# mLSTM output gates projected channel-major in four HGRN heads and applied by VectorE after the result transposes

## What is computed

```python
z = rmsnorm(x, norm_mix_g)
proj = z @ w_in
(ml_qk, ml_v, ml_o, ml_g, hg_q, hg_ff, hg_fb, hg_i, hg_g, gate_m, gate_h) = split_cols(proj, IN_SPLITS)
...
y_m = (head_rmsnorm(h_fwd + h_bwd, ml_norm_g) * jax.nn.sigmoid(ml_o)).astype(dt)
...
merged = sigmoid(gate_m) * (y_m @ w_branch_m) + sigmoid(gate_h) * (y_h @ w_branch_h)
x = x + merged @ w_out
```

## Time and profile before

| what | value |
|---|---|
| median of 3 runs | 2597.02 us (2594.98 to 2597.72) |
| span of the profiled execution | 2591.9 us |
| median less span | 5.1 us |
| PE busy | 2549.5 us (98%), 13936 matmuls |
| DVE, ACT, POOL busy | 1608.1, 913.1, 708.4 us |
| granted TensorE clock, mean | 0.996 |

### The profile page before, as it was taken

How to read it: one execution, slowest core, us unless ns; L and a number is a source line. 1 busy time by engine, 2 the same in 40 slices (tenths; PEclk the granted TensorE clock), 3 DMA queues, 4 the chain that set the end, 5 groups by cost and what they waited for, 6 DMA issues and landing times. The chain is left out here.

```text
span 2591.9 us, 34942 instructions
## 1 busy us (share of the span) xinstructions
PE 2549.5 (98%) x13936; PEld 2210.0 (85%) x13936; DVE 1608.1 (62%) x1811; ACT 913.1 (35%) x1109; POOL 708.4 (27%) x689
## 2 busy tenths in 40 slices
PE   7999999999999999999999999999999999999998
PEld 7888888899999999888888889977798888888887
DVE  5675552577888778553544524333437998987557
ACT  6342222233333333332223533243323433433433
POOL 2033220022221111422331001167412565563001
PEclk9999999999999999999999999999999999999999
DMA  8323334333222323434343546145514132334755
GB/s 282 116 78 130 98 114 138 122 114 100 85 91 101 106 98 98 163 121 147 130 154 122 212 130 219 34 165 194 202 34 146 66 130 98 114 114 171 284 194 180
DMA packets 185008, 349.62 MB, mean 135 GB/s; under 512 B 10283, under 2 KB 114039, under 8 KB 184848
## 3 DMA queue, kind: packets, MB, share of 16 engines
q1 hardware_dynamic: 123104, 154.44, 18.1%
q0 software_dynamic: 32896, 118.44, 13.2%
q10 hardware_dynamic: 28848, 74.52, 7.7%
HBM read 241.10 MB, written 106.27 MB: 134 GB/s over the span
## 5 line engine op out<-in xcount | busy, mean ns | idle before, releaser
L2225 PE MATMUL ps<-whi,a_hi 128*128 128x256 f32 x1024 | 295.6, 289 | 0.0
L2225 PE MATMUL ps<-whi,a_lo 128*128 128x256 f32 x1024 | 290.1, 283 | 0.0
L2225 PE MATMUL ps<-wlo,a_hi 128*128 128x256 f32 x1024 | 290.1, 283 | 0.0
L2194 PE MATMUL ps<-a_hi,whi 128*128 128x512 f32 x608 | 248.8, 409 | 0.2 <-DVE a_lo L1550 0.2
L1531 DVE TENSOR_TENSOR wlo<-raw,whi 128x2048 fp32r<-128x2048 f32 x65 | 150.1, 2309 | 142.6 <-ACT whi L943 142.4
L2194 PE MATMUL ps<-a_hi,wlo 128*128 128x512 f32 x608 | 237.8, 391 | 0.0
L2194 PE MATMUL ps<-a_lo,whi 128*128 128x512 f32 x608 | 237.4, 390 | 0.0
L2225 PEld LDWEIGHTS ps<-whi,a_hi 128*128 128x128 f32 x1024 | 196.8, 192 | 1.0 <-DVE a_lo L1920 0.4
L2225 PEld LDWEIGHTS ps<-wlo,a_hi 128*128 128x128 f32 x1024 | 196.9, 192 | 0.3 <-issue 0.2
L2225 PEld LDWEIGHTS ps<-whi,a_lo 128*128 128x128 f32 x1024 | 196.7, 192 | 0.0
L943 ACT ACTIVATE whi<-raw 128x2048 fp32r<-128x2048 f32 x65 | 124.5, 1916 | 183.4 <-PE ps L2225 111.2
(11 more groups left out here) (399 smaller groups left out, 6551.1 us busy)
## 6 DMA issues: line engine op xcount, KB each, us to landing
raw<-in_w_in SPq DMA_DIRECT2D x45, 1024.0 KB, 5.5
raw<-in_w_up SPq DMA_DIRECT2D x22, 1024.0 KB, 5.1
hg_T<-ev ACTq DMA_DIRECT2D x32, 512.0 KB, 2.9
qfb<-hg_T POOLq DMA_DIRECT2D x24, 512.0 KB, 5.7
wd<-in_w_down POOLq DMA_DIRECT2D x44, 256.0 KB, 3.5
down_weight_sums<-wd POOLq DMA_DIRECT2D x22, 512.0 KB, 4.3
hidden_T<-ga ACTq DMA_DIRECT2D x11, 1024.0 KB, 4.0
hidden_sums<-s POOLq DMA_DIRECT2D x10, 1024.0 KB, 5.0
```

Source lines behind the costliest of these rows:

```text
L2194: ins = pe.matmul(ps[:, u], W[sw][:, b.slot, k, c * P:(c + 1) * P], op[mw][:, k, t * HALF:(t + 1) * HALF], start=k == 0 and q == 0, stop=k ...
L2225: ins = pe.matmul(ps[:, u, part * BC:(part + 1) * BC], op[sw][:, k, t * P:(t + 1) * P], W[mw][:, b.slot, k], start=k == 0 and q == 0, stop ...
```

## The change

The output gates are projected channel-major, by the pieces that the q and k columns use, and stored in a new tensor `moT`. They are loaded channel-major into `mo` and, after `result_T`, DVE multiplies PSUM by `gcol` and by the gates in one instruction per half, in place of ACT's copies. `Hm` is multiplied by `rstd` alone. ACT stores the result behind `gate_unit(7)`, and in the last head behind the fifth operand tile.

```diff
-        mN = dram("ml_N", [T, 2048])
+        mN = dram("ml_N", [T, D])
+        moT = dram("ml_gates_T", [D, T])
...
-            mo = sb("mo", [P, NT, BC], F32, c)
+            mo = sb("mo", [P, 2, T], F32, c)
...
-                        pool.dma_start(mo[:], mN[:, ml_cols(j, 1)].rearrange("(c p) n -> p c n", p=P)).then_inc(m_o_ld, 16)
+                        pool.dma_start(mo[:], moT[ml_cols(j, 0), :].rearrange("(k p) t -> p k t", p=P)).then_inc(m_o_ld, 16)
...
-                put = put_n(mN, col)
+                put = put_n(mN, col) if h < ML_HEADS else put_t(moT, col - ML_HEADS * BC)
...
-                act.wait_ge(m_yt, j + 1)
-                staged = mo[:].rearrange("p c n -> p (c n)").rearrange("p (k t) -> p k t", k=2)
-                for k in range(2):
-                    o = (4 + 2 * k if last else 2 + 4 * k) * 512
-                    ins = act.activation(staged[:, k], psw[:, o:o + D], ACT.Copy, scale=gcol[:, k:k + 1])
-                    signal(act, ins, m_ytc, j * 2 + 1 + k)
-                act.dma_start(yT_d[at(rowy, BC), :].rearrange("(k p) t -> p k t", p=P), staged).then_inc(m_st, 16)
                 if not last:
                     gate_unit(7)
+                    act.wait_ge(m_ytc, j * 2 + 2)
+                    act.dma_start(yT_d[at(rowy, BC), :].rearrange("(k p) t -> p k t", p=P), mo[:]).then_inc(m_st, 16)
...
             for p in range(2, KT):
                 operand_hi(p, a_hi, a_raw, (p + 2) % KT)
+                if p == 4:
+                    act.wait_ge(m_ytc, 2 * ML_HEADS)
+                    act.dma_start(yT_d[(ML_HEADS - 1) * BC:D, :].rearrange("(k p) t -> p k t", p=P), mo[:]).then_inc(m_st, 16)
...
-                dve.wait_ge(m_og, j + 1)
                 dve.wait_ge(m_rs, j + 1)
                 for c in range(NT):
-                    ins = dve.scalar_tensor_tensor(Hm[:, c], Hm[:, c], rstd[:, 1, c:c + 1], mo[:, c], ALU.mult, ALU.mult)
+                    ins = dve.tensor_scalar(Hm[:, c], Hm[:, c], rstd[:, 1, c:c + 1], None, ALU.mult)
...
                 if not last:
                     decay_args(j + 1, 1)
+                    gated_rows(j, (2, 6))
+
+            def gated_rows(j, banks):
+
+                dve.wait_ge(m_og, j + 1)
+                dve.wait_ge(m_yt, j + 1)
+                for k in range(2):
+                    o = banks[k] * 512
+                    signal(dve, dve.scalar_tensor_tensor(mo[:, k], psw[:, o:o + D], gcol[:, k:k + 1], mo[:, k], ALU.mult, ALU.mult),
+                           m_ytc, j * 2 + 1 + k)
...
                 operand_lo(p, a_hi, a_lo, a_raw, (p + 2) % KT)
+                if p == 1:
+                    gated_rows(ML_HEADS - 1, (4, 6))
...
-                fill = iter([(half_T, bT, u, p) for u in range(4) for p in range(2)] + [(half_N, bN, u, p) for u in range(4) for p in range(2)])
+                fill = iter([(half_T, bT, u, p) for u in range(4) for p in range(2)] + [(half_N if h < ML_HEADS else half_T, bN, u, p)
+                                                                                           for u in range(4) for p in range(2)])
```

## The result

The changed kernel takes 2603.39 us (median of 7 runs, 2598.82 to 2606.59) against 2597.02 us before (7 runs, 2594.98 to 2598.98): a ratio of 1.0028, 95% interval 1.0019 to 1.0038. It is slower by more than the 0.2% that I had called the least that can be told from no change, and 0.2 us beyond the upper end of my range; the forecast was 2599.4 us. The profiled execution took 2604.82 us with a span of 2603.0. What lies around the span is thus 1.8 us, not the 5.1 us that I had inferred; the profiled execution of before, 2591.9 us of span, was a quick one (2591.9 + 1.8 = 2593.7 us, under the lowest of its seven runs).

What follows compares the result with a forecast made beforehand. PE, busy 2549.5 of 2591.9 us, was taken as the bound. Terms -3.9 + 6.8 - 0.5 = +2.4 us gave a span of 2594.3, forecast 2599.4 us with 5.1 us added; 8-in-10 range 2595.5 to 2603.2.

Steps and rivals of the forecast that it cites:

- Term 1: Projection pieces of HGRN heads 4 to 7: 512-column pieces take less PE time, -3.9 us (-5.1 to -3.2).
- longer waits for `Yc`: HGRN heads 4 to 6: PE waits 0.11 us longer after each head's last piece, losing 0.3 us.
- Rival B: HGRN projection: smaller matmul saving by the skill's fixed distance, about -1 us, sum +5.3 us, 2602.3 us; 8%.
- Term 2: Three mLSTM head boundaries: gating and decayed scores run in series on DVE, delaying PE, +6.8 us (+5.7 to +8.6).
- rival D: mLSTM head boundaries: PE's idling lowers the clock for 3 us, 1.5 us each, +4.5 us, 2603.9 us; 5%.
- Term 3: Behind the last mLSTM head: the later result store shortens PE's wait at the first L2209, -0.5 us (-1.2 to +0.6).
- its last part lands about 1.2 us sooner: Behind the last mLSTM head: with the store away, the read-back of `a_raw` has the lines for itself, 1.2 us sooner.
- rival C: Behind the last mLSTM head: the late store blocks POOL's last loads, 4 us fall on PE, +6.4 us, 2603.4 us; 8%.
- The `Hm` product: mLSTM heads: multiplying `Hm` by `rstd` alone takes hardly more than the old 5.88 us; costed at nothing.
- The base: Whole kernel: the runs' median lies 5.1 us above the profiled span of 2591.9 us; the same distance added to 2594.3.

Runs made afterwards that it cites:

- proj_only: The kernel before with only the projections of HGRN heads 4 to 7 made channel-major, gates not used: 2591.22 us, ratio 0.9980.
- filled_stall: The changed kernel with 11 extra, thrown-away PE matmuls before the wait at the three mLSTM head boundaries: 2598.57 us, ratio 1.0012 to the kernel before.
- gating_only: The changed kernel with the projections of HGRN heads 4 to 7 token-major again, gating still on DVE: 2606.33 us, ratio 1.0041 to the kernel before.
- scores_first: The changed kernel with the next head's decayed scores put before the gating on DVE for heads 0 to 2: 2592.82 us, ratio 0.9987 to the kernel before.

## Why the prediction was wrong

**Term 1, the projection pieces: right, but for its small loss.** Forecast -3.9 us, measured -4.2 us in the changed kernel and in proj_only. That is the whole gross saving of 4.2 us. The 0.3 us of longer waits for `Yc` that I took off didn't come: in front of the first keys of heads 5, 6 and 7 PE waited 0.91, 0.88 and 0.89 us where it had waited 0.87, 0.89 and 0.88 us. I had taken the time from the result transposes to these keys as fixed; it went from 9.30 to 9.26 us at head 5 and from 9.31 to 9.23 us at head 6, and no run shows why. A lone piece fell from 2.95 to 2.84 us as expected: the key transposes of head 4 stand 822.69 - 819.06 = 3.63 us apart where they stood 823.60 - 819.85 = 3.75 us. The Trainium skill ("TensorE: Matmul & The Clock Gate", section "Back-to-back issue gap"), with a fixed 2.5 ns per warm matmul, which the section calls the gap of an isolated matmul and not of a stream, would have given an estimated 1.0 us; the measurement decides, and it is four times that. Rival B is out.

**Term 2, the boundaries: the mechanism was right, the price was half.** The chain was as I had laid it out. The stall itself is 2.48 us longer per boundary instead of 2.21 to 2.28: I had put 0.04 us between gating and scores where 0.21 us pass while DVE clears a semaphore (the row `L155 ISA`, which stands in the order of both kernels and in the wait "0.21" of the earlier trace rows); the rest is in the two releases, 0.13 us from PE to DVE and 0.15 us back where I had 0.10 and 0.09. That makes 7.5 us instead of 6.8. Both bounds of the term were also 0.2 to 0.4 us wider than their own conditions give: gating of 1.12 us each makes 3 x 1.96 = 5.9 us, and of 1.5 us each 3 x 2.72 = 8.2 us, since a tenth more of `Hm` still fits into the free 0.6 us.

**The step that failed is the pricing of the clock at nothing, with 5% for rival D.** The profiled execution lost 7.0 us to it at the three boundaries, and filled_stall shows that it was PE's idling that brought it: same chain, same start of the product, 0.44 us of idling instead of 2.93, full clock three times out of three. My ground was one row: a stretch with a 2.6 us wait that kept 1.00. One such row shows that a wait of that length can go by, not that it does. In the changed kernel the very same wait for `kN` was followed by a lower clock:

```profile
1074.00:1079.00 5.00, 4.88 (x29) 0.66 0.02 6
```

and in the kernel before the wait of 1.8 us in HGRN head 1, one of the seven in the earlier trace rows, was too:

```profile
566.00:574.00 8.00, 6.42 (x27) 5.69 (x28) 5.71 (x4) 5.61 (x4) 0.32 (x1) 0.79 0.67 223
```

I hadn't looked at the stretch behind each wait, only behind two. The price that I gave rival D, 1.5 us per boundary, was about what gating_only shows (1.5 and 1.7 us), and less than the changed kernel's 1.7, 2.6 and 2.7 us. With that price taken as likely at each of three boundaries, 4.5 us, the sum would have reached 2603.9 us.

**Term 3, behind the last head: wrong sign, small.** Forecast -0.5 us, measured +0.6 us up to the first product with the mLSTM results, and 1.6 us more in the lower clock behind its wait (0.72 over 6 us):

```profile
1442.00:1448.00 6.00, 4.55 (x13) 3.67 (x14) 3.45 (x4) 5.78 (x8) 1.71 (x4) 0.72 1.03 409
```

The step "its last part lands about 1.2 us sooner" failed. ACT took that part at 1421.74 before and at 1432.27 after, 15.65 and 15.15 us behind the first product of `branch_first`: 0.5 us sooner. What the store didn't carry away earlier it carried later, together with `b_raw`. ACT waited for tile 1 of it and made its copies of the banks behind that tile, and PE waited for the copies:

```profile
1432.27 1.06 ACT L1155 ACTIVATE a_hi<-a_raw 128x1024 fp32r<-128x1024 f32 x1 [2.97 <-DMA a_raw<-branch_T]
1433.36 0.38 ACTq L1313 DMA_DIRECT2D branch_T<-mo  x1
...
1441.62 1.06 ACT L1155 ACTIVATE b_hi<-b_raw 128x1024 fp32r<-128x1024 f32 x1 [1.53 <-DMA b_raw<-branch_T]
1442.70 2.48 ACT L949 ACTIVATE ev<-ps 128x512 f32<-128x512 f32 x4
```

The store did leave late and POOL did issue tiles 6, 7 and the merge gates late (1441.62), as rival C had it. No stall came of that: ACT still idled for 4.33 us in front of its next copies, at 1465.15. The cost came from the first tiles, not the last, and it went when the store was issued one tile earlier: 19.52 us from the result transposes to that product against 20.11 before is the small gain that I had forecast.

**The `Hm` product: right to cost nothing.** It took 2.20 us (2.98 us at the third boundary) instead of 5.88, and nothing was gained by it, since PE set the time of the transposes.

**The base.** The sum stood against a profiled span that was 3 us quicker than the median run, and I carried the difference along as if it lay around the span. In medians this hid 3.3 us of what the sum lacked: against its own base the forecast 2594.3 missed the span of 2603.0 by 8.7 us, of which the boundary clock is 7.0, the longer stall 0.7 and term 3 1.1; term 1 gave 0.3 more than forecast, and the clock stretches elsewhere (-0.8, +1.6, +1.6, -2.2) add 0.2.

## What to carry to other kernels

Where PE is busy throughout, a stall has two prices: its own length, which the chain of waits gives, and what the clock takes behind it, which it doesn't; look at the granted clock behind every wait of the trace, not one, and add the mean. When work moves to an engine that waits for the same event, put everything that doesn't need the event in front of it: here that turned 1.0028 into 0.9987. A change that is a gain in one part and a loss in another should be timed in its parts before it is kept or dropped.

## What the hardware showed that I had not expected

The clock falls behind quite short idling, and not each time. Idling of 2.93 us was followed by a lower clock at five of the six boundaries of the changed kernel and gating_only; the 2.6 us in front of the first scores in five of the eight profiled kernels; the 1.7 to 1.8 us in HGRN head 1 in six of the eight, the changed kernel not among them; the 0.73 to 0.77 us at the nine boundaries of scores_first and the two kernels built on it never. The wait in front of the first product with the mLSTM results was followed by it where it was 2.23 us (changed), 2.11 us (gating_only) and 1.86 us (proj_only), and not where it was 2.19 us (filled_stall) or 2.06 us (scores_first). What decides between these cases stays open.

DVE and POOL were slower side by side than alone, with tiles in SBUF on both sides. In the changed kernel two DVE instructions of 1024 elements (L1727 and L1729 in the fence of DVE at the first boundary), 1.22 us each before, when POOL was idle, took 1.95 and 2.18 us, while POOL's took 2.25 and 2.02 us instead of 1.31 and 1.05 us as later in the head. Before:

```profile
1158.30 1.22 DVE L1728 TENSOR_TENSOR Em<-Em,icol 128x1024 f32<-128x1024 f32 x1
```

and with the change:

```profile
1150.56 1.50 POOL L806 TENSOR_TENSOR kw<-kN,hcol 128x512 f32<-128x512 f32 x1 [1.70 <-ACT kN L1137]
1152.03 2.25 POOL L800 TENSOR_TENSOR qw<-mq,wrow 128x512 f32<-128x512 f32 x1
1154.24 2.02 POOL L806 TENSOR_TENSOR kw<-kN,hcol 128x512 f32<-128x512 f32 x1
...
1167.68 1.31 POOL L800 TENSOR_TENSOR qw<-mq,wrow 128x512 f32<-128x512 f32 x1
1168.93 1.05 POOL L806 TENSOR_TENSOR kw<-kN,hcol 128x512 f32<-128x512 f32 x1
```

The two DVE instructions and the three of POOL take 2 x 1.22 + 1.05 + 1.31 + 1.05 = 5.85 us if one adds up what each takes alone; here they filled the 5.70 us from 1150.56 to 1156.26, as if they had taken turns. Before, the same POOL work lay beside the `Hm` product, which took 5.88 us with it and 3.26 us in the last head, where POOL did nothing at the time. Making `Hm` shorter moved the collision to the next instructions, so at the first boundary DVE gained 2.0 us up to the end of the decay arguments, not the 3.7 us by which `Hm` itself shrank. I saw this in profiles only and made no run for it.
